# One program for the in-projection and the gated recurrence of a linear attention layer, against two programs in a row

## What is computed

```python
z = hn @ w_in                                    # hn: normed residual
q, k, v, g, a = jnp.split(z, [nk, 2 * nk, 2 * nk + nv, 2 * nk + 2 * nv], axis=-1)
logit = (a @ w_gate2 + b_gate).astype(jnp.float32)
la = (jax.nn.log_sigmoid(logit) / GLA_TAU)       # per token and key column
...
b = jnp.cumsum(la, axis=1)                       # inside a block of 64 tokens
qd = q * jnp.exp(b)
kd = k * jnp.exp(-b)
a = jnp.einsum('blhk,bshk->bhls', qd, kd)
a = jnp.where(jnp.tril(jnp.ones((L, L), dtype=bool)), a, 0.0)
o = jnp.einsum('blhk,bhkv->blhv', qd, s) + jnp.einsum('bhls,bshv->blhv', a, v)
b_last = b[:, -1]
s_new = s * jnp.exp(b_last)[..., None] + jnp.einsum(
    'bshk,bshv->bhkv', k * jnp.exp(b_last[:, None] - b), v)
...
o = o * lax.rsqrt(jnp.mean(o * o, axis=-1, keepdims=True) + EPS)
return (o * jax.nn.silu(g)) @ w_out, s_fin       # o times norm_g, added to the residual
```

## Time and profile before

| | us |
|---|---|
| Median of three runs | 3243.76 |
| Lowest and highest | 3236.13 and 3247.28 |
| The profiled execution | 3243.13 |
| Its span | 3241.4 |

### The profile page before, as it was taken

How to read it: one execution, slowest core, us unless ns; L and a number is a source line. 1 busy time by engine, 2 the same in 40 slices (tenths; PEclk the granted TensorE clock), 3 DMA queues, 4 the chain that set the end, 5 groups by cost and what they waited for, 6 DMA issues and landing times. The chain is left out here.

```text
span 3241.4 us, 48505 instructions
## 1 busy us (share of the span) xinstructions
PE 2950.6 (91%) x19428; PEld 2791.7 (86%) x19428; DVE 1303.8 (40%) x2395; ACT 918.1 (28%) x1679; POOL 999.6 (31%) x655
## 2 busy tenths in 40 slices
PE   6899789796999999999889999994969999999997
PEld 6899667595999999999878887863959999999996
DVE  5111143516656555211323434343166555652114
ACT  3000244303322223210324434343033232332112
POOL 1221022314444345542221212101134444445420
PEclk9999776796999999999989999997969999999998
DMA  8523232302222223421312324336022222235211
GB/s 146 127 83 96 76 107 73 108 2 98 65 82 66 78 79 118 166 83 40 122 44 88 108 87 142 100 95 215 7 86 77 79 65 82 68 107 182 88 40 59
DMA packets 328252, 294.39 MB, mean 91 GB/s; under 512 B 23248, under 2 KB 306976, under 8 KB 327280
## 3 DMA queue, kind: packets, MB, share of 16 engines
q1 hardware_dynamic: 323168, 282.11, 28.8%
q10 hardware_dynamic: 4880, 9.44, 0.8%
HBM read 211.47 MB, written 95.76 MB: 95 GB/s over the span
## 5 line engine op out<-in xcount | busy, mean ns | idle before, releaser
L143 PE MATMUL f_ps<-f_x_hi,f_w_hi 128*128 128x288 f32 (+1 forms) x2976 | 932.1, 313 | 58.7 <-POOL f_x_lo L917 28.4
L144 PE MATMUL f_ps<-f_x_hi,f_w_lo 128*128 128x288 f32 (+1 forms) x2976 | 927.4, 312 | 0.0
L145 PE MATMUL f_ps<-f_x_lo,f_w_hi 128*128 128x288 f32 (+1 forms) x2976 | 925.1, 311 | 0.0
L143 PEld LDWEIGHTS f_ps<-f_x_hi,f_w_hi 128*128 128x128 f32 x2976 | 565.2, 190 | 65.9 <-issue 24.2
L145 PEld LDWEIGHTS f_ps<-f_x_lo,f_w_hi 128*128 128x128 f32 x2976 | 567.3, 191 | 0.0
L144 PEld LDWEIGHTS f_ps<-f_x_hi,f_w_lo 128*128 128x128 f32 x2976 | 566.4, 190 | 0.0
L904 POOL TENSOR_TENSOR f_w_lo<-f_w_whole,f_w_hi 128x512 fp32r<-128x512 f32 x136 | 188.7, 1396 | 391.8 <-DVE f_w_whole L1156 172.5
L1233 DVE TENSOR_TENSOR res<-res,f_ps 128x384 f32<-128x384 f32 x192 | 106.4, 554 | 457.7 <-PE f_ps L145 457.7
L1179 DVE TENSOR_TENSOR res<-f_ps,res 128x288 f32<-128x288 f32 x308 | 140.3, 458 | 209.2 <-PE f_ps L145 200.0
L143 PE MATMUL in_ps<-in_x_hi,in_w_hi 128*128 128x384 f32 x600 | 202.7, 338 | 21.8 <-POOL in_w_lo L137 20.2
L1179 DVE TENSOR_TENSOR f<-f_ps,f 128x288 f32<-128x288 f32 x308 | 139.9, 457 | 160.1 <-PE f_ps L145 149.8
(11 more groups left out here) (283 smaller groups left out, 5619.1 us busy)
## 6 DMA issues: line engine op xcount, KB each, us to landing
f_x_whole<-hid_rows SPq DMA_DIRECT2D x44, 576.0 KB, 5.0
f_raw<-in_ffn_w_down SPq DMA_DIRECT2D x48, 384.0 KB, 3.4
gla_rows<-in_sums SPq DMA_DIRECT2D x24, 576.0 KB, 3.2
res_rows<-res SPq DMA_DIRECT2D x3, 4608.0 KB, 15.9
in_stage<-in_gla_w_in SPq DMA_DIRECT2D x25, 512.0 KB, 4.5
hid_rows<-f SPq DMA_DIRECT2D x44, 288.0 KB, 2.5
hid_rows<-res SPq DMA_DIRECT2D x44, 288.0 KB
f_raw<-in_ffn_w_gate SPq DMA_DIRECT2D x22, 512.0 KB, 3.9
```

The source lines that it names most:

```text
L143: pe.matmul(out, w_hi, x_hi, start=first, stop=False)
L144: pe.matmul(out, w_lo, x_hi, start=False, stop=False)
L145: return pe.matmul(out, w_hi, x_lo, start=False, stop=last)
```

## The change

`Segment`, `project` and `gla_core` go, and `mixer` takes their place. It is one program of 36 *slots*, one for each tile of each head, behind an opening. The opening projects `a`, the values of head 0 and, group by group, its logits, decays, keys and queries. In a slot TensorE makes the scores, the state update and the output of its tile, and between them and behind them the projection groups that `FILL_PLAN` names: gate groups `g` of the slot's own head, keys, queries and values of the next. Values and gates are now made with tokens on the partitions, 128 tokens by 256 columns a group; keys and queries stay 384 tokens wide. In the last head a slot has one gate group. `LOGITS` puts the decays of a third of the next head's tokens at the ends of slots 2, 5 and 7. The outputs of a finished head, three a slot, are gated in slots 0 to 2 of the next, turned on TensorE, and sent by SP through a ring of three buffers to `o_rows` in memory. Projected values, gates, keys, queries and outputs lie in the place of the residual, which SP first writes to `res_rows` (the spill). `gla_rows` goes, and the output product runs with `reload`.

The diff, cut to its core:

```diff
-class Segment:
...
-def project(nc, S, tag, gain, segments, aside=None):
...
-def gla_core(nc, S, a):
...
+def mixer(nc, S, a, tag):
...
+    FILL_PLAN = ("g0g1g2", "g3g4g5", "g6g7g8", "k0q0", "v0v1v2", "v3v4v5", "k1q1", "v6v7", "k2v8q2")
+    def items_of(s):
+        h, i = at_slot(s)
+        if h == H - 1:
+            return [("g", h, i)]
+        text = FILL_PLAN[i]
+        out = [(text[c], h if text[c] == "g" else h + 1, int(text[c + 1])) for c in range(0, len(text), 2)]
+        return out
+    BEGIN = [("a", 0, t) for t in range(NG)] + [("v", 0, i) for i in range(NT)] + \
+        [(kind, 0, t) for t in range(NG) for kind in "kq"]
+    ITEMS = BEGIN + [x for s in range(SLOTS) for x in items_of(s)]
...
+    def units_of(s):
+        h, i = at_slot(s)
+        more = h + 1 < H
+        return {0: [("g", h, 0), ("g", h, 1)], 1: [("k", h + 1, 0)] if more else [], 2: [("q", h + 1, 0)] if more else [],
+                3: [("v", h + 1, c) for c in range(2)] if more else []}.get(i, [])
...
+    LOGITS = {2: 0, 5: 1, 7: 2}
+    def fills_of(s):
+        h, i = at_slot(s)
+        out = []
+        if i < NG and h:
+            out += [("o", (h - 1) * NT + NG * i + n) for n in range(NG)]
+        if i in LOGITS and h + 1 < H:
+            out.append(("l", NG * (h + 1) + LOGITS[i]))
+        if s + 1 < SLOTS:
+            out.append(("k", s + 1))
+        return out
...
+            v = flat[:, :2 * TOK].rearrange("p (i d) -> p i d", d=VW)
+            gate = flat[:, 2 * TOK:4 * TOK].rearrange("p (i d) -> p i d", d=VW)
+            o = flat[:, 4 * TOK:6 * TOK].rearrange("p (i d) -> p i d", d=VW)
+            kq = flat[:, 6 * TOK:].rearrange("p (n t) -> p n t", t=TOK)
...
+                for x in UNITS[:ST]:
+                    fetch(x)
+                keep_strips(sp, S)
+                sp.dma_start(w2[:], a["gla_w_gate2"][0]).then_inc(small_in, 16)
+                sp.dma_start(bg[:], a["gla_b_gate"].rearrange("l (h p) -> p (l h)", p=P), allow_slow_non_contiguous=True
+                             ).then_inc(small_in, 16)
+                sp.dma_start(ng[:], a["gla_norm"].rearrange("l (n p) -> p (l n)", p=P), allow_slow_non_contiguous=True
+                             ).then_inc(small_in, 16)
+                sp.dma_start(S.res_rows, S.res[:]).then_inc(spilled, 16)
+                for x in UNITS[ST:5]:
+                    fetch(x)
+                load_states(0)
+                for s in range(SLOTS):
+                    h, i = at_slot(s)
+                    for x in units_of(s):
+                        fetch(x)
+                    if h and i == 0:
+                        send_states(h - 1)
+                        load_states(h)
+                    for x in fills_of(s):
+                        if x[0] == "o":
+                            send_mixed(x[1])
...
+                make_k2(0)
+                for s in range(SLOTS):
+                    h, i = at_slot(s)
+                    if i == SAMPLE:
+                        spread_queries(h)
+                        for n in range(DEC_B):
+                            spread_keys(h, n)
+                    for x in units_of(s):
+                        split_unit_(x)
+                    if s + 1 < SLOTS:
+                        make_k2(s + 1)
...
+                for x in BEGIN[:HELD]:
+                    piece(x, 0, DK)
+                norm.sum_all(pe)
+                norm.spread_all(pe)
+                for x in BEGIN[HELD:NG + NT]:
+                    piece(x, 0, DK)
+                for t in range(NG):
+                    pe.wait_ge(norm.kept, NG)
+                    fill(("l", t))
+                    for x in BEGIN[NG + NT + 2 * t:NG + NT + 2 * t + 2]:
+                        piece(x, 0, DK)
+                fill(("k", 0))
+                for s in range(SLOTS):
+                    h, i = at_slot(s)
+                    run = items_of(s)
+                    fills = fills_of(s)
+                    scores(s)
+                    if i < SAMPLE:
+                        update(s)
+                    if run:
+                        piece(run[0], 0, 4)
+                    out(s)
+                    if i == SAMPLE:
+                        for n in range(DEC_B):
+                            if n == 4 and run:
+                                piece(run[0], 4, 6)
+                            update_stream(h, n)
+                    if run:
+                        piece(run[0], 6 if i == SAMPLE else 4, DK)
+                    for n in range(max(len(run) - 1, len(fills))):
+                        if n < len(fills):
+                            fill(fills[n])
+                        if n + 1 < len(run):
+                            piece(run[n + 1], 0, DK)
+                for i in range(NT):
+                    fill(("o", (H - 1) * NT + i))
...
+                norm.round(act, 0)
+                for x in UNITS[:1]:
+                    round_weights(x)
+                for t in range(1, NG):
+                    norm.round(act, t)
+                for x in UNITS[1:3]:
+                    round_weights(x)
+                norm.squares(act)
+                norm.root(act)
+                norm.keep(act)
+                act.wait_ge(norm.inverse, 1)
+                act.wait_ge(spilled, 16)
+                for x in UNITS[3:5]:
+                    round_weights(x)
...
+                    if i == 0 and h:
+                        root(h - 1)
+                    for x in units_of(s):
+                        round_weights(x)
+                    square(s)
+                    for n in range(max(len(run), len(fills))):
+                        if n < len(run) and run[n][0] == "v":
+                            take_v(run[n])
+                        if n < len(run) and run[n][0] == "g":
+                            take_gate(run[n])
+                        if n < len(fills):
+                            take(fills[n])
+                    for x in fills:
+                        if x[0] == "l":
+                            decays(x[1])
+                root(H - 1)
+                for i in range(NT):
+                    take(("o", (H - 1) * NT + i))
...
+                for t in range(NG):
+                    decays(t)
+                    scales(t)
+                    take_kq(("k", 0, t))
+                    take_kq(("q", 0, t))
+                for s in range(SLOTS):
+                    h, i = at_slot(s)
+                    mask(s)
+                    if i < SAMPLE:
+                        step(s)
+                    if h and i < NG:
+                        for n in range(NG):
+                            gate_out((h - 1) * NT + NG * i + n)
+                    keep_out(s)
+                    if i == SAMPLE:
+                        for n in range(DEC_B):
+                            step_stream(h, n)
+                    for x in items_of(s):
+                        if x[0] in "kq":
+                            take_kq(x)
+                    for x in fills_of(s):
+                        if x[0] == "l":
+                            decays(x[1])
+                            scales(x[1])
+                for i in range(NT):
+                    gate_out((H - 1) * NT + i)
...
-        S.gla_rows, S.o_rows = dram("gla_rows", [GLA_IN, TOK]), dram("o_rows", [D, TOK])
+        S.o_rows = dram("o_rows", [D, TOK])
...
-            with ExitStack() as phase:
-                operands(nc, S, phase, "in")
-                project(nc, S, "in", G_MIX0, [(w_in, 0, body // P, None, S.gla_rows, 0, 0),
-                                              (w_in, GLA_IN - P, 1, None, S.gla_rows, body, P - RANK)],
-                        aside=keep_strips)
-            with nc.sbuf_tensor("gla_mixed", [P, DK, TOK], F32) as S.mixed:
-                gla_core(nc, S, a)
-                add_product(nc, S, "go", a["gla_w_out"][0])
+            mixer(nc, S, a, "mix")
+        with nc.sbuf_tensor("gla_mixed", [P, DK, TOK], F32) as S.mixed:
+            add_product(nc, S, "go", a["gla_w_out"][0], reload=True)
```

More of the change, by code:

```diff
@@ new lines, in sums_bank, with turn_bank, is_taken, weights @@
+            def sums_bank(x):
+                n = PLACE[x]
+                place = (gps[:, 0], gps[:, 1], sps[:], ops[:], ups[:, 0], ups[:, 1])[n] if n < HELD else gps[:, n % 2]
+                return place[:RANK if x[0] == "a" else P, :width(x)]
+            def turn_bank(x):
+                return tps[:, FILL[x] % 2, :]
+            def is_taken(engine, x):
+                engine.wait_ge(taken[FILL[x] % 2], FILL[x] // 2 + 1)
+            def weights(x):
+                kind, _, half = x
+                if kind in "vg":
+                    return wv_hi[:, half, :], wv_lo[:, half, :]
+                n = (DK * RANK) if kind == "a" else D
+                slot = 1 if kind == "q" else 0
+                return w_hi[:, slot, :n], w_lo[:, slot, :n]
@@ L1472, in finish @@
-                def finish(h):
-                    pe.wait_ge(added, h * NT + (NT + 2))
```

(32 more changed lines are left out.)

988 lines of the change are left out of this document (451 added, 537 removed).

## The result

The changed kernel takes 3307.86 us (median of four runs, 3305.62 to 3309.11) against 3240.9 us of the kernel before (median of four). The ratio is 1.0205, with a 95% interval of 1.0184 to 1.0225. The forecast was 3320 us with a range of 3268 to 3375. The profiled execution spans 3306.2 us.

A forecast was written before the change was run, and what follows sets the result against it. TensorE bounds in-projection (almost gapless) and recurrence (gaps, clock 0.74). 185 + 375 + 75 + 25 + 17.7 + 34.5 = 712 us to the output product's first matmul, against 635.3: 77 later, so 3320 us, range 3268 to 3375.

The forecast's parts named there:

- Opening: Before the heads: value weights queue behind strips and residual copy, the norm behind them; first scores near 185 us.
- Work in the heads: TensorE's pure work in the heads, projections and tile steps together: 375 us.
- Waits in the heads: TensorE's stops in the heads for masks behind decays, weight splits, gate weights and turned keys: 75 us.
- its sign: In slots 3, 6 and 8, TensorE's output matmuls wait 4 to 6 us for the mask, nine times.
- The gate weights': Gate weights are rounded only after the last value group: waits of 3.2 us a head, 5.5 at the first.
- the keys behind the value weights' split: In slot 3 GpSimd splits two value weight tiles ahead of the next turned keys: 1.7 us a head.
- The late takes: Turned keys taken late in the heads: 1.6 us a head, and 7 in the last head.
- Clock: Lower granted clock after ten stops in the heads, some 2.5 us each: 25 us, bounds 17 and 50.
- Closing: Last head's nine outputs gated, turned and sent, 17.7 us; then loads to the output product's first matmul, 34.5 us.
- The opening isn't held up: Rival: transfers share the engines, the tile lands by 45, scores start near 118; 67 us less, 3253 us; chance 0.06.
- The clock stays low: Rival: many stops keep the heads' clock at a mean of 0.8, costing 94 us, not 25: 3389 us; chance 0.09.
- Interleaving works in the slots: Rival: the decays' chain is covered, the heads' waits and clock loss go: 75 + 25 us less, 3220 us; chance 0.08.

The follow-up runs named there:

- strips_late: Changed kernel with the 6 MB write of the bias strips moved in SP's order from the opening to slot 4 of the first head: 3246.95 us.
- norm_first: Changed kernel with the norm's squares and sums ahead of the late second half of the value weights: 3293.46 us in one run.
- best0: Changed kernel with strips_late, mask_first2, gate_w, the residual loaded behind the mixed rows, and the first head's gate weights prepared behind the opening's value groups: 3149.42 us.
- grouped: Changed kernel with the next head's value groups from slots 4, 5, 7 and 8 all in slot 8: 3309.1 us in one run.
- mask_first: Changed kernel with a slot's mask and state step on VectorE ahead of the decays of the slot before: 3279.37 us.
- mask_first2: mask_first, plus GpSimd preparing the next tile's keys ahead of splitting weights, and the third decay chain moved from slot 7 to 6: 3249.19 us.
- gate_w: Changed kernel with a head's last value group ahead of its last key group in the last slot: 3297.09 us.
- best_bare: best0 with the value groups of slots 4, 5, 7 and 8 all in slot 8: 3166.88 us.

## Why the prediction was right, step by step

- **Opening**, forecast 185 us for the first scores, measured 176.33. The mechanism was right, and strips_late and norm_first show it. The size was 9 us too large. The strips landed near 91.4 (27.21 and 64.2 us to landing), as forecast (92), but the small loads, the copy and the tile behind them took 13 us and not 18: the late weights were rounded at 104.53, half a microsecond ahead of the bound of 105. The norm followed (128.59 for about 135, so that its copies came at 123.55 to 128.11 and not after 130). The three rounds of logits, decays, keys and queries took 28 us, as forecast.
- **Work in the heads**, forecast 375 us. best0's 395 us less 17 of idle time leave 378, and a clock of 0.99 accounts for some 4 of these. The output of a tile, estimated at 1.1, takes 1.2 (238.69 to 239.90 in grouped).
- **Waits in the heads**, forecast 75 us, measured as TensorE's idle time 66.3 (472.87 less 406.56). For the mask, slot 5's were forecast at 4 and took 3.7, slot 7's at 4.9 and took 4.6 to 4.7, slot 2's at 5.3 in the first head and took 5.1, but at 6.1 in the next two, where they took 3.2 and 4.7; why these are shorter stays open. All nine came, four of them under the 4 us that the prediction named as its sign. The gate weights' were 13.6 for 15.1. The 1.7 us a head for the keys behind the value weights' split didn't show, since the mask's wait in the same slot covered it; with that gone it was 6.1 to 6.5, as mask_first shows. This term was mis-sized: it counts the split alone and not ScalarE's chain ahead of it. The late takes were put at 1.6 us a head, but the sum leaves the first head's out; no such wait came in that head.
- **Clock**, forecast 25 us (17 to 50). TensorE is busy 406.56 us in the heads and 377.74 in best0, for the same 2581 records at a clock of 0.99, so the clock cost some 29. The nine stops for the mask gave back 21.9 of it (mask_first2), the three short ones for the gate weights about 2.8 (gate_w).
- **The heads in all**, forecast 375 + 75 + 25 = 475 us, measured 472.87. That this is so near is partly luck: the waits were put 9 us too high, and work and clock together 7 us too low.
- **Closing**, forecast 17.7 and 34.5 us, measured 48.8 together, of which 34.7 from the loads' start, so that the last outputs took 14.
- **The rivals.** "The opening isn't held up" fell with the trace after. "The clock stays low" fell with the clock of 0.92. "Interleaving works in the slots" was wrong for this order of instructions, but its mechanism exists: with the mask ahead of the decays, later groups do cover the chain, and 58.7 us come back. Its price of 100 us was too high, since the waits for the gate weights and the late keys have other causes. The Trainium skill ("Perfetto Trace Analysis", Optimization Strategy) says that interleaving may improve performance where the most-contended engine changes over time. That condition isn't met here: TensorE is the busiest engine in both stretches of the earlier trace rows (264.21 of 267 us and 192.99 of 218), which differ in clock and in gaps. So the rule did not make this rival the forecast, though the prediction says that it does.
- What the prediction did not ask is what interleaving brings where nothing waits. For the value groups that were moved it is, by the traces, some 6.6 us in the changed kernel (grouped) and 20.3 in the mended one (best_bare, 17.5 by the medians). The gate, key and query groups stayed between the steps in every run, so the worth of all interleaving isn't shown. Of the 91 us that best0 gains on the kernel before, about 12 are the attention's product and up to 9.35, with some clock behind them, the strips. Up to the product's first matmul TensorE is busy 463 us in best0 and 527.5 before, at a mean clock of 0.93 and 0.85. Which part of that is the clock, kept up by dense work between the steps, and which is less work (values and outputs with tokens on the partitions) was not separated; that the stores and loads of the projected rows are gone was not tried alone either.

## What to carry to other kernels

A large transfer that nothing needs soon belongs behind the loads that the next stage waits for: here its place in one queue was worth 61 us. In a program written out slot by slot, a long chain over several engines should stand behind the short step that TensorE waits for, and whoever moves it should look at what was queued behind it on every engine, since these are the next waits. Before dense work is put between steps, look at whether the steps already cover one another, and compare the stretch that changed in the traces, since a few microseconds there are lost in the scatter of single totals.

## What the runs showed of the hardware

That a stop of about 4 us costs some 2.5 us more through the clock was expected from the earlier trace rows. The nine stops of 3.2 to 5.1 us cost 2.4 us more on the average, the three of 2.87 us only 0.9. A change of ScalarE's function table takes 1.28 us, and the function starts 0.01 us behind it (218.33 + 1.28, 219.62): no drain is to be seen, as in the earlier trace rows. The Trainium skill ("ScalarE: Activation LUTs", What ACT_TABLE_LOAD costs) has a drain of about 1380 ns behind each; here the rows decide against it. The time that the prediction gave by that page, 3332 us, is also further from the 3308 measured than its own 3320, but other terms were off by as much in all, so the total alone would not decide it.
